# A fused decoder step on one core: the first expert pair's operand built by TensorE from marks, and an end with halves of columns and LN passes on GpSimd

## The reference, cut to what matters

```python
x1 = _layernorm(ALPHA * x + mix, ln1_g, ln1_b)
# _hier_moe: top-1 group of 4, then top-2 of its 8 experts
for e in range(N_EXPERTS):                      # 32 experts
    gu = xt @ w_gate_up[e]                      # (1024, 512)
    h = jax.nn.silu(gu[:, :D_EXPERT]) * gu[:, D_EXPERT:]
    y = y + gate[:, e:e + 1] * (h @ w_down[e])  # (256, 1024)
out = _layernorm(ALPHA * x1 + ffn, ln2_g, ln2_b)
```

## Time and profile before

| | |
|---|---|
| runs shown | 596.06, 596.57, 598.97 us, median 596.57 |
| profiled execution | 594.66 us; its span 593.0 us, 1.66 us around it |
| busy in the span | PE 87%, DVE 63%, ACT 32%, POOL 23% |
| granted TensorE clock, mean | 0.989 |
| DMA | 157.95 MB moved, mean 266 GB/s |

### The profile page before, as it was taken

How to read it: one execution, slowest core, us unless ns; L and a number is a source line. 1 busy time by engine, 2 the same in 40 slices (tenths; PEclk the granted TensorE clock), 3 DMA queues, 4 the chain that set the end, 5 groups by cost and what they waited for, 6 DMA issues and landing times.

```text
span 593.0 us, 8961 instructions
## 1 busy us (share of the span) xinstructions
PE 515.9 (87%) x3296; PEld 279.5 (47%) x3296; DVE 372.8 (63%) x722; ACT 190.9 (32%) x356; POOL 134.4 (23%) x156
## 2 busy tenths in 40 slices
PE   6999999999989879999999898888887667767762
PEld 5887788874355533455457743332332222222220
DVE  0752049898954577643178665678886567756686
ACT  0100375204244642140232122445444334432340
POOL 1001045510026740000000202333323231221231
PEclk9999999999999999999999999999999999999997
DMA  8950008580607832002978599999999999999951
GB/s 302 385 187 6 1 0 318 194 312 1 253 34 293 345 142 61 2 35 102 425 279 328 198 422 414 402 398 418 415 416 410 420 416 419 415 414 419 405 203 46
DMA packets 34298, 157.95 MB, mean 266 GB/s; under 512 B 12712, under 2 KB 12712, under 8 KB 20304
## 3 DMA queue, kind: packets, MB, share of 16 engines
q1 hardware_dynamic: 20880, 127.46, 53.7%
q0 software_dynamic: 10752, 29.59, 13.2%
q10 hardware_dynamic: 2624, 0.34, 0.4%
HBM read 160.12 MB, written 21.23 MB: 306 GB/s over the span
## 4 chain that ended last, share of the span: by engine, by line
PE 58%; DMA 24%; DVE 7%; ACT 6%; issue 3%; SPq 1%; POOL 0%; DVEq 0%; POOLq 0%; ACTq 0%
DMA arena_o<-in_w_gu 19%; PE ps L496 17%; PE ps L968 8%; PE ps L752 8%; PE ps L991 4%; PE ps L597 3%; PE ps L659 2%; PE ps L643 2%; PE ps L917 2%; PE ps L680 2%; DMA first_rows<-arena_s,known 1%; PE ps L815 1%; DMA known<-slot_table 1%; PE ps L563 1%; DMA slot_table<-arena_s 1%
## 5 line engine op out<-in xcount | busy, mean ns | idle before, releaser
L968 PE MATMUL ps<-arena_w,arena_s 128*64 128x512 f32 x368 | 107.6, 595 | 25.2 <-DMA arena_o<-in_w_gu 11.7
L496 PE MATMUL ps<-arena_w 128*128 128x260 f32 x416 | 95.4, 390 | 5.4 <-DMA arena_w<-in_xT 4.8
L496 PEld LDWEIGHTS ps<-arena_w 128*128 128x128 f32 x416 | 79.9, 194 | 20.4 <-DMA arena_w<-in_xT 5.6
L968 PEld LDWEIGHTS ps<-arena_w,arena_s 128*64 128x64 f32 x368 | 32.8, 137 | 96.9 <-issue 66.8
L991 PE MATMUL ps<-arena_w,cs 128*64 128x512 f32 x184 | 56.5, 618 | 20.8 <-ACT cs L1267 20.8
L752 PE MATMUL ps<-arena_o,arena_s 128*128 128x512 f32 x128 | 58.2, 600 | 0.8 <-DVE arena_s L1612 0.8
L968 PE MATMUL ps<-arena_o,arena_s 128*64 128x512 f32 x112 | 50.2, 595 | 0.0
L1484 DVE STREAM_TRANSPOSE arena_s<-arena_w 128x1024 f32<-128x1024 f32 x36 | 42.1, 1217 | 8.1 <-PE ps L597 8.1
L2161 POOL DMA_INDIRECT first_rows<-arena_s,known x15 | 18.0, 1199 | 113.2 <-ACT arena_s L1274 104.3
L1921 DVE TENSOR_TENSOR arena_s<-arena_s,ps 128x256 f32<-128x256 f32 x16 | 6.7, 421 | 56.0 <-ACT arena_s L1263 56.0
L991 PEld LDWEIGHTS ps<-arena_w,cs 128*64 128x64 f32 x184 | 16.2, 140 | 51.1 <-issue 30.4
(11 more groups left out here) (349 smaller groups left out, 894.9 us busy)
## 6 DMA issues: line engine op xcount, KB each, us to landing
arena_w<-in_w_gu SPq DMA_DIRECT2D x46, 1024.0 KB
arena_w<-in_w_dn SPq DMA_DIRECT2D x23, 1024.0 KB
arena_o<-in_w_gu SPq DMA_DIRECT2D x14, 1024.0 KB
arena_o<-in_w_dn SPq DMA_DIRECT2D x7, 1024.0 KB
arena_w<-in_w_in SPq DMA_DIRECT2D x12, 512.0 KB, 13.5
arena_o<-in_w_out SPq DMA_DIRECT2D x1, 4096.0 KB, 13.7
arena_s<-in_w_gu SPq DMA_DIRECT2D x4, 1024.0 KB, 7.8
first_rows<-in_x_tok SPq DMA_DIRECT2D x1, 2080.0 KB, 19.2
```

Source lines behind the costliest of these rows:

```text
L496: last = mm(ps[rows, b + n, 0:HALF], lhs(k), rhs(k)[:, n * HALF:(n + 1) * HALF], start=(k == 0), stop=(k == ks - 1))
L968: last = mm(ps[64 * e:64 * e + 64, 2 + q, :], xgT[:, k, CAP * e:CAP * (e + 1)], gu_w[2 * slots + e][:, k, :], start=(k == 0), stop=(k == K ...
```

## The change

Two parts. **Start.** The first pair's operand is no longer gathered and turned. DVE makes first_mark, for each token and each of the first pair's 128 slots a 1 where the token has that slot (experts 0 and 16 of the one-hot arrays, e = 0::NPAIR); PE multiplies every x1 tile by it and sums over the five tiles in PSUM (first_tokens, 5 x 8 matmuls). logits(4) goes to bank 5. In place of keep_warm(9), first_tokens(0) to (2) stand ahead of the last ranks. tokens_out(0) on DVE and ACT moves ahead of the gate work; hidden(0) and tokens_out(1) move into the payload loop; PE runs experts(0) before it waits for routed and makes the facts. SP loads slot 4 behind the last x1 store without other waits; lng and lng2 wait for x1_stored and xt_ps. POOL gathers pairs 1 and 0 first, pairs 2 and 3 after xt_ps. **End.** For pair 14 POOL gathers the other part before it scatters its own, and runs the LayerNorm passes; for pair 15 own part and statistics go by halves of the columns as PE finishes each half; PE gets five filler matmuls after the last products. Core of the diff:

```diff
-            return ps[:, 6, 0:NL] if m < 2 else ps[:, m % 2, 0:NL]
+            return ps[:, 6 if m < 2 else 5 if m == TT - 1 else m % 2, 0:NL]
 # SP
-            landed(sp, x1_stored, TT)
-            landed(sp, gathered[0])
             for half in range(2):
                 gate_up(4, slice(4, 5), half)
             down(4, slice(4, 5))
+            landed(sp, x1_stored, TT)
+            sp.wait_ge(xt_ps, 1)
             sp.dma_start(lng, ...)
 # PE
             logits(4)
-            pe.wait_ge(slots_ready, 1)
+            def first_tokens(m):
+                t, n = ORDER[m], ROWS[ORDER[m]]
+                pe.wait_ge(ln_norm, m + 1)
+                for k in range(KD):
+                    last = mm(ps[:, k // 4, (k % 4) * P:(k % 4 + 1) * P], x1[0:n, t, k * P:(k + 1) * P], first_mark[0:n, m, :],
+                              start=(m == 0 and k % 4 == 0), stop=(m == TT - 1), skip_group_check=True)
+                return last
+            pe.wait_ge(lg_out, TT)
             ranks(TT - 1, range(TT - 1))
             totals(range(TT - 1))
-            slot_numbers(range(TT - 1))
-            keep_warm(9, 4)
+            for m in range(3):
+                first_tokens(m)
+            keep_warm(3, 4)
             pe.wait_ge(route_dve, 2)
             ranks(TT - 1, [TT - 1])
             totals([TT - 1]).then_inc(rank_ps, 1)
-            keep_warm(4, 4)
+            first_tokens(3)
+            pe.wait_ge(slots_ready, 1)
+            slot_numbers(range(TT - 1))
             pe.wait_ge(slots_ready, 2)
             slot_numbers([TT - 1]).then_inc(slots_ps, 1)
-            keep_warm(28, 4)
+            first_tokens(4).then_inc(xt_ps, 1)
...
-            turn_tokens(None, 0)
-            first = products(None, 0)
+            experts(None, 0, *products(None, 0))
             pe.wait_ge(routed, 1)
...
-            experts(None, 0, *first)
 # ACT: tokens_out(None, 0) ahead of the two Exp; hidden(None, 0) ahead of act.wait_ge(routed, 1)
 # DVE
+            def mark_first(a, b):
+                link(tt(in_first[:, 1, :, a:b], ...))
+                link(stt(in_first[:, 2, :, a:b], ...))
+                return tt(first_mark[:, a:b, :].rearrange("p t (e c) -> p t e c", e=2), ..., ALU.is_equal)
...
             rank_of(0, 4)
-            mark_slots(0, 4).then_inc(slots_ready, 1)
+            step(mark_first(0, 4))
             logits_out(4)
...
             number_parts(4, TT)
+            first_known(4, TT)
+            mark_slots(0, 4).then_inc(slots_ready, 1)
             dve.wait_ge(rank_ps, 2)
             rank_of(4, TT)
+            step(mark_first(4, TT))
             mark_slots(4, TT).then_inc(slots_ready, 1)
...
+                if c == 2:                       # payload loop, 7 steps
+                    hidden(None, 0)
+                    tokens_out(None, 1)
...
+            def finish_on_pool(it, n):           # pair 14: other part, statistics, mean_done; no passes
+            def finish_last(it, n):
+                stt(x, yo[2], k[:, 3:4], x, ALU.mult, ALU.add).then_inc(finish_step, 1)
+                dve.wait_ge(root_done, nth(it, n))
+                V.reciprocal(stat[:, 2:3], stat[:, 2:3]).then_inc(finish_step, 1)
+                for h in range(2):
+                    dve.wait_ge(dn_ps, nth(it, n, add=1 + h))
+                    stt(half, ps[:, 5 + h, :], k[:, 2:3], half, ALU.mult, ALU.add).then_inc(own_added, 1)
+                    V.bn_stats(bn[:, h, :], half).then_inc(finish_step, 1)
+                V.bn_aggr(mv[:, 0, 0:2], bn[:, :, :]).then_inc(mean_done, 1)
+                stt(x, x, mv[:, 0, 0:1], lng2[:, 0, :], ALU.subtract, ALU.mult).then_inc(finish_step, 1)
+                V.reciprocal(mv[:, 0, 2:3], mv[:, 0, 2:3]).then_inc(finish_step, 1)
+                stt(x, x, mv[:, 0, 2:3], lng2[:, 1, :], ALU.mult, ALU.add).then_inc(out_ready, 1)
 # POOL
-            for n in range(4):
+            for n in (1, 0, 2, 3):
+                if n == 2:
+                    pool.wait_ge(xt_ps, 1)
                 gather_rows(n, first_at[:, n:n + 1])
...
+            pool.wait_ge(finish_step, added)     # yo[0] free: pair 12's other part is added
             gather_other((past,), n)             # n = 14, now ahead of pair_step(14)
+            pair_step((past,), n)
+            gather_other((past,), n + 1)
+            scatter_out((past,), n - 1)
+            pool.wait_ge(finish_step, scaled)
+            step(G.tensor_scalar(x, x, stat[:, 0:1], stat[:, 2:3], ALU.subtract, ALU.mult))
+            step(G.tensor_tensor(x, x, lng2[:, 0, :], ALU.mult))
+            step(G.tensor_tensor(x, x, lng2[:, 1, :], ALU.add))
+            send_out(n)
+            pool.wait_ge(out_ready, ready)
+            send_out(n + 1)
```

More of the change, by code:

```diff
@@ L238, in hymba_step @@
         first_at = part(arena_s, S_TAB + NF * NPAIR, NPAIR).bitcast(I32)
+        first_mark = part(arena_s, S_E, TT, P)
+        in_first = part(arena_s, S_E + TT * P, 3, 2, TT)
         turn_i = part(arena_s, S_RT + 260, 2, TT).bitcast(I32)
@@ L975, in products, with experts @@
                     turn_tokens(it, n + 1)
+                else:
+                    for _ in range(5):
+                        mm(ps[:, 7, 0:P], ident[:, :], ident[:, :], start=True, stop=True)
                 return slots, landed_count
-            def experts(it, n, slots, landed_count):
+            def experts(it, n, slots, landed_count, last_pair=False):
                 pe.wait_ge(h_ready, nth(it, n, add=1))
@@ L992, in experts @@
                                       dn_w[2 * slots + e][:, f, h * 512:(h + 1) * 512], start=(f == 0), stop=(f == 1))
+                    if last_pair and h == 0:
+                        last.then_inc(dn_ps, 1)
                 last.then_inc(dn_ps, 1)
-            turn_tokens(None, 0)
-            first = products(None, 0)
+            experts(None, 0, *products(None, 0))
             pe.wait_ge(routed, 1)
@@ L1012, in _ @@
                     experts(it, n, *products(it, n))
-            for n in range(HEAD + BODY, NPAIR):
-                experts((past,), n, *products((past,), n, n == NPAIR - 1))
+            for n in range(HEAD + BODY, NPAIR - 1):
+                experts((past,), n, *products((past,), n))
+            experts((past,), NPAIR - 1, *products((past,), NPAIR - 1, True), True)
         @block.scalar
@@ L1253, in tokens_out @@
                 last.then_inc(xt_act, 1)
+            tokens_out(None, 0)
             act.wait_ge(route_dve, 3)
@@ L1258, in _ @@
             fn(rs[:, 6:8, :], rs[:, 6:8, :], ACT.Exp).then_inc(route_act, 1)
-            tokens_out(None, 0)
             def hidden(it, n, last_pair=False):
@@ L1294, in _ @@
             for n in range(HEAD):
-                hidden(None, n)
+                if n > 0:
+                    hidden(None, n)
                 if n == 0:
@@ L1817, in _, with tokens_out, hidden @@
             stt(first_at[:, :], work[:, 1, :], -1.0, work[:, 2, :], ALU.add, ALU.add).then_inc(first_ready, 1)
+            def tokens_out(it, n):
+                dve.wait_ge(xt_ps, nth(it, n, add=1))
+                if n > 0:
+                    dve.wait_ge(gu_ps, nth(it, n))
+                for k in range(KD // 2):
+                    last = ts(xgT[:, k, :], ps[:, k // 4, (k % 4) * P:(k % 4 + 1) * P], vec[:, V_LG + k:V_LG + k + 1],
+                              vec[:, V_LB + k:V_LB + k + 1], ALU.mult, ALU.add)
+                last.then_inc(xt_sb, 1)
+            def hidden(it, n):
+                dve.wait_ge(silu_done, nth(it, n, add=1))
+                tt(hx, sg, ps[:, 2 + n % 2, DE:2 * DE], ALU.mult).then_inc(h_ready, 1)
+            tokens_out(None, 0)
             link(V.tensor_reduce(rs[:, 3, :], L[:, :, 0:NG], AX_X, ALU.max))
@@ L1847, in _ @@
             link(tt(later[:, 1, :], turn_f[:, 1, :], turn_f[:, 0, :], ALU.is_gt))
-            def tokens_out(it, n):
-                dve.wait_ge(xt_ps, nth(it, n, add=1))
-                if n > 0:
-                    dve.wait_ge(gu_ps, nth(it, n))
-                for k in range(KD // 2):
-                    last = ts(xgT[:, k, :], ps[:, k // 4, (k % 4) * P:(k % 4 + 1) * P], vec[:, V_LG + k:V_LG + k + 1],
-                              vec[:, V_LB + k:V_LB + k + 1], ALU.mult, ALU.add)
-                last.then_inc(xt_sb, 1)
-            tokens_out(None, 0)
             g, flat = gate.rearrange("p n t -> p (n t)"), rest.rearrange("p n t -> p (n t)")
@@ L1873, in _ @@
                     step(last)
+                if c == 2:
+                    hidden(None, 0)
+                    tokens_out(None, 1)
             last.then_inc(facts_ready, 1)
@@ L1967, in finish @@
                 stt(x, x, stat[:, 2:3], lng2[:, 1, :], ALU.mult, ALU.add).then_inc(out_ready, 1)
+            def finish_on_pool(it, n):
+                x = xg[ring(n)]
+                dve.wait_ge(own_added, nth(it, n, add=1))
+                dve.wait_ge(yo_landed[n % 2], nth(it, n + 1, 2, 16))
```

(12 more changed lines are left out.)

78 lines of the change are left out of this document (51 added, 27 removed).

## The result

The changed kernel takes 606.45 us (median of four runs, 604.40 to 610.11), the one before beside it 597.77 us: the medians are 8.7 us apart, and over all runs the ratio is 1.0155 with the interval [1.0118, 1.0191]. The forecast was 600.7 us, 4.1 us slower, and a range up to 602.8. The sign was right, and so were the place that bounds the start and the wait that takes over there. The size was more than twice what was forecast, and the result lies outside the range: the LayerNorm passes on POOL cost 9.5 us instead of 5.0, and a half clock behind PE's wait had no term at all. The profiled execution took 604.40 us, span 602.8 us against 593.0 us: +9.8 us.

A forecast was written before the change was run, and what follows sets the result against it. Bound: PE and slots until the refill behind products(3), then weight bytes. Start 0.3 + 0.95 + 3.2 = +4.4 us, less 0.3 latency, +4.1; end 0.0; so 600.7 us on the median, range 596.0 to 602.8.

The forecast's parts named there:

- The bound: Until the refill behind products(3), PE and slots bound the kernel, then bytes; slot 4's 7.2 us head start gains nothing.
- Start of products(0): First products on PE start at 338.7 instead of 338.36 us: +0.3, bounds -1.4 and +2.0.
- the dip: Half clock on PE for some 3.4 us from about 324 us, in first_tokens, costing 1.7 us.
- Rival (a): Clock keeps its full level in first_tokens: products(0) 1.7 us earlier, +2.4 in all, 599.0 us; 17%.
- Facts behind experts(0): On PE, the facts now stand behind experts(0) and delay products(1) by 0.95 us.
- thin cover: Slack for DVE's hidden(0) and routed, 0.4 and 1.4 us; if it fails, PE slips by the excess.
- The wait for the table: ACT waits for table_stored in front of hidden(1), so Silu(1) comes 3.2 us late, at P0 (start of products(0)) + 24.8.
- Rival (c): Thin covers fail, hidden(0) or routed 1 to 2 us late, or a second dip: +5.5 to +6.5, 602.6 us; 10%.
- The end: Last pairs' halves and LayerNorm on POOL (5.0 us with waits) end at about 588.5 against 588.52: gain 0.0.
- The end's bound of 1.5 us lost: Worst case at the end: DVE and POOL each wait in full for the other twice, 1.5 us lost.
- The lock: At the end, DVE's first two-operand SBUF pass waits until POOL's passes end, 588.5 instead of 586.8 us undisturbed.
- - 0.3: Up to 0.3 us of transfer latency given back at the refill, whose first bytes came into a just emptied queue.

The follow-up runs named there:

- the run with fillers: Kernel after the change, with 14 small unused matmuls on PE between products(1) and the wait for h of pair 1: 603.27 us, ratio 1.0102.
- the run with two steps: Kernel after the change, with subtraction and multiplication of POOL's first LayerNorm pass in two instructions: one execution, 607.03 us.

## Why the prediction was wrong in size, by its steps

The step that failed is the end: its term of 0.0 rested on 5.0 us for POOL's three passes, and they took 9.5, so the end cost 3.5 us. In the start two more terms were wrong, a half clock behind PE's wait that had no term (2.7 us) and the start of products(0) (+0.3 forecast, -2.4 measured), and they cancel, which is luck.

**The bound: right.** Time follows the refill behind products(3), and the head start of slot 4 runs into a queue that goes dry. The DMA view of the kernel after shows zeros from 381.6 to 386.8, and with the load 11.8 us later nothing changes. This step decided the sign.

**Start of products(0): the term +0.3 was wrong by 2.7 us.** Forecast: 17.7 us behind the last logits, since "that stretch stays ... so I keep the dip". Measured 15.03, -2.4 against before, in the kernel after and in seven of the ten experiments with the changed start; 16.3 with one half clock of 3.4 us in first_tokens, 18.3 with two (two runs). In all eight with 15.03 a half clock began between 308 and 313 us, ahead of the last logits, and none followed before 360; the other three had none there. Rival (a) came true for the profiled run, and even beyond its size: the 1.7 us of the dip, and another 1.0 us that I had added up too generously, half of it before the end of first_tokens(4), half behind it (1.64 us to products(0) where I had kept 2.13). The dip was not saved but moved: it now lies ahead of the logits, where it is most of their +0.9.

**Facts behind experts(0): right.** 0.95 us forecast, 1.15 measured (three runs: 45.25 to 45.28 against 44.12). Neither thin cover failed.

**The wait for the table: the place was right and the time nearly, a term was missing.** Silu(1) was forecast at P0 + 24.8 and came at P0 + 25.8: table_stored came 0.6 us later (its issue by 0.4, and the DMA took 7.01 us instead of 6.58, less 0.2 that the forecast had too much), and ACT's two loads took 0.4 us longer (rows_at 0.76 instead of 0.46). Against before, Silu(1) is 5.2 us later, 4.1 without the facts (forecast 3.2). What I did not ask is what PE does while it waits. It idles for 4 us and then gets half the clock for 6.8 us, 2.7 us of time on experts(1), as the run with fillers shows. From before to after: -2.4 (P0), +5.2 (Silu(1)), -0.7 (turn_tokens(2) is done while PE waits, so the copy behind Silu(1) comes sooner: Silu(1) to products(3) takes 18.98 us in the run with fillers, 19.72 before), +2.7 (the clock) = +4.8 on the refill, against +4.4 forecast. The sum nearly fits because two errors, P0 and the clock, cancel: luck, not a good forecast. Rival (c) had named a second dip, but in first_tokens and not behind a wait. The refill, forecast for 386 to 387, was requested at 388.26.

**The end: the term 0.0 was wrong by 3.5 us.** Step by step: POOL's start was forecast 11.3 us behind the second half of products(15) and came 12.4 behind it, since the gather of the other part was issued 0.85 us later relative to the stream. POOL's passes, forecast at 1.12 and two of 1.89 us, took 3.78, 2.34 and 3.20. The first price came from a row that multiplies twice; this one subtracts, and a subtraction costs 3.7 us. The second came from a tensor_tensor of another place and length in the same rows, 1919 ns for 1040; here 1024 with an operand from arena_o take 2.34 alone. Why these two differ no run tells. The Trainium skill (GPSIMD Engine Reference, elementwise side by side) has 4497 ns for 2048 elements of such an operation, from which I had the estimate of 2.25 us and left it for the row; with 2.34 measured it was nearer. The end's bound of 1.5 us lost allowed for engines waiting on each other, not for a dearer instruction. In the forecast POOL was done 2.8 us ahead of DVE (585.7 against 588.5); in the run it ends 2.2 us behind DVE's 595.21, and two scatters then go one after the other, 1.37 us.

**The lock: half right.** I had read the earlier trace rows as a wait over several POOL instructions. Here DVE's pass at 591.99 ends at 595.21, 1.09 us behind the end of the one tensor_tensor beside which it started (594.12), and the next of POOL's then takes 0.86 us longer. In the run with two steps DVE's pass starts beside the multiplication and takes 1.95 us, and ends 1.06 us behind the multiplication's end. That is the rule of the Trainium skill (SBUF — State Buffer, two separate sides): the ports are held for one instruction, and the later one waits. These rows agree with the page. The earlier trace rows do not: DVE's instruction there starts at 116.64 beside the second of POOL's four and ends at 120.87, 0.57 us behind the last of them (120.30), so it did wait over three. Those four follow each other without a gap, while the passes at the end stand 0.08 us apart, each waiting for the one before it; whether that makes the difference no run tells. My reading of the row was right, and carrying it over to the end was the error. And DVE's pass at 590.59 starts while POOL's subtraction, which reads SBUF too, has 1.1 us to go, and takes its plain 1.28 us (so does the one at 592.09 in the run with two steps); by the page it should have waited, and the measurement decides. On the path the lock cost 0.9 us here, against the 1.7 us that I had charged to it.

**Sum.** Forecast +4.4 - 0.3 + 0.0 = +4.1. Measured +0.9 (logits, the clock's) + 4.9 + 0.4 (within what that stretch varies) + 3.5 = +9.7 on the profiled runs; the medians are 8.7 us apart, and by the ratio it is 0.0155 x 596.57 = +9.2.

## What to carry to other kernels

A step that PE can take earlier pushes another one back; follow the pushed one to the engine that waits for it in order, and ask what is queued behind that wait: here a load that nobody needed yet stood in front of Silu, and moving three lines undid it. When a wait makes PE idle for some microseconds, add the half clock behind it to its price (here 4 us of idling, then 2.7 us), or fill the gap with matmuls. Before crediting a change with a shorter stretch, look whether a half clock only moved out of it. Price an instruction on POOL by a row with the same operation, not only the same form and size, and let a pass go to POOL only if it is off the path even at three times its price.

## What the runs showed of the hardware

- GpSimd's tensor_scalar over 128 x 1024 float32 takes 1.12 us for a multiplication or an addition, 1.19 for two multiplications by scalars of the partition, and 3.71 to 3.78 with a subtraction.
- At the end of the kernel a VectorE pass with two SBUF operands was held back beside GpSimd's tensor_tensor (3.22 us instead of 1.28) and beside its multiplication (1.95), and not beside its subtraction (1.28, twice). Earlier in the kernel, beside four tensor_tensors in a row, such an instruction was held until all four were done (4.23 us instead of 0.69).
- TensorE's granted clock fell to one half behind 3.1 to 4.0 us of idling in eight of eight profiled runs, for 6.8 us (3.4 in one), and cost 2.7 us over 16 matmuls; with small matmuls in the gap it stayed full.
- TensorE's half clock in first_tokens depends on the run: absent in eight of eleven profiled runs with the changed start, once or twice in the other three, with a cost of 1.2 to 1.6 us each. A forecast for one run can't know it; a range can.
